# Two of a norm's modulation tiles multiplied on TensorE instead of VectorE, and small loads and position tables moved

## Chip, cores, metric

One NeuronCore of a Trainium2 chip. The metric is the device time of one execution in microseconds. Before the change: 3044.1 us, the median of 3 runs (3043.52 to 3049.18).

## What is computed

Two transformer blocks on 256 tokens of width 2048, in float32. The first block's modulation and first norm matter here:

```python
c_act = jax.nn.silu(c)
mod = (c_act @ ada_w[l] + ada_b[l]).reshape(B, N_MOD, D)[:, :, None, :]
shift_m, scale_m, gate_m, shift_f, scale_f, gate_f = [mod[:, i] for i in range(N_MOD)]
h = rmsnorm(x, norm_mix_g[l]) * (1.0 + scale_m) + shift_m
x = x + gate_m * token_mix(h, cos, sin, w_in[l], ...)
```

`c_act` is one vector of 2048; `ada_w` is 2048 by 12288. `shift_m` and `scale_m` are its first 4096 columns: eight tiles of 512. `cos` and `sin` come from `positions` and are used in the attention of `token_mix`. The second block attends to a memory `mem` of 256 rows, whose keys and values (`rmsnorm(mem) @ w_mem_kv`, one set for each of its two layers) the kernel computes first.

## The kernel before

The five engines run five programs that are written out by hand and wait for each other by semaphores. Activations lie with features on the partitions: `x`, `h_hi`, `h_lo` are [128, 16 chunks, 256 tokens].

**Weights.** All large weights pass in pieces of 1 MB (four chunks of 128 rows by 512 columns, or as much) through a ring of four slots, `w_raw`. SyncE issues the loads in the order of use; each waits (`free_slot`) until what lay in its slot has been consumed. The table `PRODUCTS` gives this order, and with it what each engine does: a product (`gla_q`, ...) is a matrix product of so many tiles of 512 columns, each of four pieces. A piece is cut in two by ScalarE (`w_hi`, a rounded copy, L1220, two halves of 1.05 us) and VectorE (`w_lo`, the rest, L1534), into two pairs of buffers; TensorE (all its matmuls pass through `mm`, L819) then makes three passes, hi by hi, lo by hi, hi by lo: 48 matmuls of 256 columns for a piece. A first cut can be put inside a norm that comes before it, by the table `CUT_IN_NORM` (norm, and chunk behind which piece e is cut).

**Modulation.** In mode "A" (`ada0`: three tiles, `ada1`: one) and as a rider between the pieces of other products, a piece of `ada_w` is multiplied by `c_act` on VectorE (`ada_piece`, L1584 and L1591, four operations of 128x512 for a piece, four pieces for a tile), into `probs_t`. `ada_total` on TensorE then sums it over the partitions by four matmuls of one column against ones, into PSUM `bank[3]`. `take_mod` (L1603) adds `ada_b`, `gain` (L1609) makes `gain_eff`. The first norm (called `mix`) needs the eight tiles 0 to 7: three of ada0, four riders on mem_k0, mem_v0, mem_k1, mem_v1, and ada1.

**The head, in order.** SyncE: `const` (L694), sixteen loads of small vectors into `vec_rows` (L705), `mem_rows`, `x_rows`, then the ring. POOL loads the positions. TensorE transposes `vec_rows` (L992), then `mem_rows` in four steps (`to_features`, L1003), sums the squares of the memory (norm mem0), transposes x in four steps, and goes to product mem_k0. ScalarE and VectorE copy the transposes out of PSUM. VectorE also makes the arguments of sine and cosine (`tables(0)`, L1782 to L1793; the sines are ScalarE's, L1362 and L1363) before its first copy. VectorE then multiplies four pieces of ada0, scales `mem_t` by the root (L1664), and in `apply("mem0")` writes `h_lo` two chunks at a time (L1668) with one of the other eight pieces of ada0 between them. Then follow the products mem_k0, mem_v0, (norm mem1) mem_k1, mem_v1 with a rider on each piece; behind them ada1, `take_mod(0, 8)`, `gain`, and `apply("mix")`, which writes h chunk by chunk (L1679, L1315 on ScalarE, L1687) with the first cuts of gla_q inside. Then gla_q, gla_gk (one piece), gla_k, and the rest of the two blocks.

Of the kernel before, what the change touches and what calls it, by code (L numbers as in the profile page):

```python
# [132 lines left out]
class Product:  # L133
# [18 lines left out]
    def ada_tiles(self, n):  # L152
# [36 lines left out]
CUT_IN_NORM = {"mem_k1": ("mem1", {0: -1, 1: -1, 2: 7, 3: 12}), "gla_q": ("mix", {0: 1, 1: 4, 2: 9, 3: 13}),  # L189
# [6 lines left out]
BEFORE = {"split": [0], "plain": [0], "ada": [0]}  # L196
_in_slot = [0] * 4
_p = _s = _t = _a = 0
for _i, _g in enumerate(PRODUCTS):

    _g.r0, _g.p0, _g.s0, _g.t0, _g.a0 = len(LANDED), _p, _s, _t, _a
    for _k in range(_g.tiles * _g.slots):
        _ada = _g.mode == "A" or (_g.rider > 0 and _k % (_g.rider + 1) == _g.rider)
        _in_slot[len(LANDED) % 4] += 16 * (1 if _ada else _g.dmas)
        LANDED.append(_in_slot[len(LANDED) % 4])
        KIND.append("ada" if _ada else "split" if _g.split else "plain")
        for _kind, _is in (("split", _g.split and not _ada), ("plain", not _ada), ("ada", _ada)):
            BEFORE[_kind].append(BEFORE[_kind][-1] + _is)
# [4 lines left out]
    _a += _g.ada_tiles(_g.tiles)  # L213
    _g.p1, _g.t1 = _p, _t
# [69 lines left out]
def program(nc, A, out):  # L284
    with ExitStack() as ctx:
# [124 lines left out]
        angles = at("angles", small[0] - 4 * KB, [P, 3, S])  # L410
# [61 lines left out]
        ada_done = sem("ada_done")  # L472
        ada_sum = sem("ada_sum")
# [137 lines left out]
        def ada_buffer(g, a):  # L611

            return a % 2 if g.rider == 1 else 0
# [78 lines left out]
        def _(sp):  # L692
            x_in, mem_in = A["x"][0], A["mem_2"][0]
            sp.dma_start(const[:], A["const"]).then_inc(ld_const, 16)  # L694
            n_vec = 0
            for name, (at0, w) in VECTORS.items():
                v = A[name]
                v = v.rearrange(" ".join(f"a{k}" for k in range(len(v.shape))) + " -> (" +
                                " ".join(f"a{k}" for k in range(len(v.shape))) + ")") if len(v.shape) > 1 else v
                v = v.rearrange("(r p) -> r p", p=P)  # L700
                done = 0
                while done < w:
                    r, t = (at0 + done) % P, (at0 + done) // P
                    n = min(P - r, w - done)
                    sp.dma_start(vec_rows[r:r + n, t, :], v[done:done + n]).then_inc(ld_vec, 16)  # L705
                    n_vec += 1
                    done += n
            assert n_vec == N_VEC_DMA
# [49 lines left out]
            for name in ("ada0", "mem_k0", "mem_v0", "mem_k1", "mem_v1", "ada1"):  # L758
# [32 lines left out]
        def _(pool):  # L791
# [21 lines left out]
            positions("positions_2")  # L813
# [3 lines left out]
        def _(pe):  # L817
# [61 lines left out]
            def ada_total(g, i, tb):  # L879

                a, n = g.a0 + tb // g.rider, g.ada_tiles(g.body)
                pe.wait_ge(ada_done, 4 * (a + 1) + per(i, 4 * n))
# [3 lines left out]
                last.then_inc(ada_sum, 1)  # L886

# [133 lines left out]
            product("mem_k0", *h, chunk_ready=as_normed("mem0"), between=[lambda: ada_total(G["ada0"], 0, 2)])  # L1021
# [1102 lines left out]
```

## Time and profile before

| | |
|---|---|
| time, median of 3 runs | 3044.1 us (3043.52 to 3049.18) |
| span of the profiled execution | 3058.3 us, 14.2 above that median; no other time of that execution is listed |
| TensorE busy, with matmuls | 2842.3 us, 93% |
| VectorE busy | 1830.9 us, 60% |
| ScalarE busy | 1196.0 us, 39% |
| mean granted TensorE clock | 0.961 of 2.4 GHz |
| modulation pieces on VectorE (L1591) | 360 operations, 270.2 us busy, 751 ns each |
| read from memory | 561.95 MB, 185 GB/s over the span |

The busy shares are means over the whole span; the first 7% of it, where the change lies, is different. PEld is TensorE's loading of weights, which overlaps its matmuls; an f32 matmul counts as two instructions in the profile. SPq is SyncE issuing a load. A PEclk of 0.50 is 1.2 GHz, 1.00 is 2.4 GHz.

### The profile page before, as it was taken

Reading aid. Unit: us, or ns where it says so; the run is one execution under the profiler, and the core shown is the slowest. Engines: PE = TensorE matmul, PEld = TensorE weight load, DVE = VectorE, ACT = ScalarE, POOL = GpSimd, SP = SyncE. Lnnn points to the kernel's source line nnn. Section 1 sums busy time; section 2 is a strip of 40 time slices with the busy share of each in tenths; the row PEclk is TensorE's granted clock in tenths of the full one; section 3 lists DMA queues with packets and bytes.
Section 4 is the critical chain, followed back from the end, with each engine's and each line's share of the span. In section 5 each row is a group of like instructions: output and inputs, shape, how many; then the busy total and the mean of one; then the engine's idle time right before and its main releaser. Section 6 shows DMA issues by size and latency. Waiting matters only on the chain.

```text
span 3058.3 us, 50651 instructions
## 1 busy us (share of the span) xinstructions
PE 2842.3 (93%) x21461; PEld 2720.1 (89%) x21461; DVE 1830.9 (60%) x2283; ACT 1196.0 (39%) x1508; POOL 5.7 (0%) x14
## 2 busy tenths in 40 slices
PE   3979988999999999989999999998997989899988
PEld 2879867999999779989999999997997989899888
DVE  6795665766765557764544444445556556646754
ACT  3435332343343433343333333333444344544533
POOL 0000000000000000000000000000000000000000
PEclk7989998999999979999999999998999999999988
DMA  7786822778767327745555555553553545654222
GB/s 266 280 305 232 289 91 70 260 250 284 253 235 210 90 101 257 260 162 196 176 182 183 184 183 178 178 180 110 180 186 127 174 142 189 197 179 152 83 84 95
DMA packets 319752, 568.32 MB, mean 186 GB/s; under 512 B 21961, under 2 KB 61217, under 8 KB 318962
## 3 DMA queue, kind: packets, MB, share of 16 engines
q1 hardware_dynamic: 318354, 561.73, 54.8%
q0 software_dynamic: 1248, 4.46, 0.4%
q8 instruction: 111, 1.82, 0.3%
q14 instruction: 39, 0.32, 0.0%
HBM read 561.95 MB, written 4.19 MB: 185 GB/s over the span
## 4 chain that ended last, share of the span: by engine, by line
PE 82%; DVE 13%; issue 3%; ACT 2%; DMA 1%; SPq 0%; DVEq 0%; ACTq 0%
PE tile_ps L819 74%; PE misc_ps L819 6%; DVE w_lo L1534 4%; DVE probs_t L1591 1%; ACT w_hi L1220 1%; DVE rstd L1641 0%; PE misc_ps L963 0%; DVE o_tmp L1978 0%; DVE stats L1753 0%; DVE x L1956 0%; DVE tile_ps L1874 0%; DVE gla_att L1877 0%; DVE o_lo L1738 0%; PE tile_ps L1003 0%; DMA w_raw<-in_w_mem_kv 0%
## 5 line engine op out<-in xcount | busy, mean ns | idle before, releaser
L1534 DVE TENSOR_TENSOR w_lo<-w_raw,w_hi 128x1024 fp32r<-128x1024 f32 x866 | 1021.4, 1221 | 890.1 <-ACT w_hi L1220 889.1
L1220 ACT ACTIVATE w_hi<-w_raw 128x1024 fp32r<-128x1024 f32 x866 | 867.7, 1050 | 1161.4 <-PE tile_ps L819 1120.2
L819 PE MATMUL tile_ps<-h_hi,w_hi 128*128 128x256 f32 x4208 | 695.9, 287 | 54.5 <-DVE w_lo L1534 33.5
L819 PE MATMUL tile_ps<-h_hi,w_lo 128*128 128x256 f32 x4208 | 687.3, 285 | 0.0
L819 PE MATMUL tile_ps<-h_lo,w_hi 128*128 128x256 f32 x4208 | 686.5, 284 | 0.0
L819 PEld LDWEIGHTS tile_ps<-h_hi,w_hi 128*128 128x128 f32 x4208 | 589.4, 193 | 64.5 <-issue 35.1
L819 PEld LDWEIGHTS tile_ps<-h_hi,w_lo 128*128 128x128 f32 x4208 | 587.7, 193 | 0.0
L819 PEld LDWEIGHTS tile_ps<-h_lo,w_hi 128*128 128x128 f32 x4208 | 587.6, 193 | 0.0
L1591 DVE SCALAR_TENSOR_TENSOR probs_t<-w_raw,c_act,probs_t 128x512 f32<-128x512 f32 x360 | 270.2, 751 | 10.9
L819 PE MATMUL tile_ps<-o_hi,w_hi 128*128 128x256 f32 x1024 | 168.5, 287 | 12.3 <-DVE w_lo L1534 7.5
L819 PE MATMUL tile_ps<-o_hi,w_lo 128*128 128x256 f32 x1024 | 166.2, 285 | 0.0
L819 PE MATMUL tile_ps<-o_lo,w_hi 128*128 128x256 f32 x1024 | 166.1, 285 | 0.0
L819 PEld LDWEIGHTS tile_ps<-o_hi,w_hi 128*128 128x128 f32 x1024 | 143.4, 195 | 14.9 <-DVE w_lo L1534 9.8
L819 PEld LDWEIGHTS tile_ps<-o_lo,w_hi 128*128 128x128 f32 x1024 | 142.9, 194 | 0.0
L819 PEld LDWEIGHTS tile_ps<-o_hi,w_lo 128*128 128x128 f32 x1024 | 142.9, 194 | 0.0
L819 PE MATMUL tile_ps<-sw_hi,w_hi 128*128 128x256 f32 x704 | 113.7, 284 | 1.7 <-DVE w_lo L1534 1.5
L819 PE MATMUL tile_ps<-sw_hi,w_lo 128*128 128x256 f32 x704 | 113.1, 283 | 0.0
L819 PE MATMUL tile_ps<-sw_lo,w_hi 128*128 128x256 f32 x704 | 113.1, 283 | 0.0
L819 PEld LDWEIGHTS tile_ps<-sw_hi,w_hi 128*128 128x128 f32 x704 | 97.1, 192 | 2.7 <-DVE w_lo L1534 2.7
L819 PEld LDWEIGHTS tile_ps<-sw_lo,w_hi 128*128 128x128 f32 x704 | 97.1, 192 | 0.0
L819 PEld LDWEIGHTS tile_ps<-sw_hi,w_lo 128*128 128x128 f32 x704 | 97.1, 192 | 0.0
L819 PE MATMUL tile_ps<-w_hi,h_hi 128*128 128x512 f32 x224 | 70.7, 397 | 0.0
(330 smaller groups left out, 2314.2 us busy)
## 6 DMA issues: line engine op xcount, KB each, us to landing
w_raw<-in_ada_w SPq DMA_DIRECT2D x96, 1024.0 KB, 5.2
w_raw<-in_w_in SPq DMA_DIRECT2D x89, 1024.0 KB, 5.1
w_raw<-in_ffn_w_in SPq DMA_DIRECT2D x88, 1024.0 KB, 5.0
w_raw<-in_w_out SPq DMA_DIRECT2D x48, 1024.0 KB, 5.1
w_raw<-in_ffn_w_down SPq DMA_DIRECT2D x44, 1024.0 KB, 5.1
w_raw<-in_b_w_in SPq DMA_DIRECT2D x33, 1024.0 KB, 5.2
w_raw<-in_a_w_in SPq DMA_DIRECT2D x32, 1024.0 KB, 5.5
w_raw<-in_w_kv SPq DMA_DIRECT2D x24, 1024.0 KB, 5.2
```

The costliest lines, as they stand in the source:

```text
L819: return nc.tensor.matmul(o, l, r, start=start, stop=stop, skip_group_check=True)
L1220: f(w_hi[s_ % 2][:, hf], w_raw[r % 4][:, hf], ACT.Copy).then_inc(cut_hi, 1)
L1534: ins = v.tensor_tensor(w_lo[s_ % 2][:, hf], w_raw[r % 4][:, hf], f32(w_hi[s_ % 2][:, hf]), ALU.subtract)
L1591: ins = v.scalar_tensor_tensor(acc, w[:, c, :], c_act[:, k:k + 1], acc, ALU.mult, ALU.add)
```

## The change

Two tiles, the first and the last of the eight, are multiplied on TensorE: `ada0` (one tile) at the start and `ada3` (one tile) behind mem_v1. A new function `ada_on_pe` uses the raw piece as weights and a column of `c_act` as the moving side, so that no sum over partitions is left: 16 matmuls of one column for a piece, accumulated in PSUM. A new semaphore `ada_by_pe` frees the ring's slots for them. The sixteen small loads move to ScalarE's queue, in front of all that ScalarE does. The first two pieces of mem_k0 are cut inside norm mem0, behind chunks 11 and 15. The tables move behind gla_q on VectorE and ScalarE, and `angles` gets a second place in memory. The modulation is taken in two steps, tiles 0 to 6 before the norm and tile 7 behind its chunk 11.

```diff
-PRODUCTS = [Product("ada0", 3, 4, split=False, mode="A", rider=1),
+PRODUCTS = [Product("ada0", 1, 4, split=False, mode="A", rider=1, on_pe=True),
+            Product("ada1", 1, 4, split=False, mode="A", rider=1),
             Product("mem_k0", 1, 4, rider=1), Product("mem_v0", 1, 4, mode="N", rider=1),
             Product("mem_k1", 1, 4, rider=1), Product("mem_v1", 1, 4, mode="N", rider=1),
-            Product("ada1", 1, 4, split=False, mode="A", rider=1),
+            Product("ada2", 1, 4, split=False, mode="A", rider=1),
+            Product("ada3", 1, 4, split=False, mode="A", rider=1, on_pe=True),
...
-CUT_IN_NORM = {"mem_k1": ("mem1", {0: -1, 1: -1, 2: 7, 3: 12}), "gla_q": ("mix", {0: 1, 1: 4, 2: 9, 3: 13}),
+CUT_IN_NORM = {"mem_k0": ("mem0", {0: 11, 1: 15}), "mem_k1": ("mem1", {0: -1, 1: -1, 2: 7, 3: 12}), "gla_q": ("mix", {0: 1, 1: 4, 2: 9, 3: 13}),
...
@@ the ring's free_slot, SyncE
-                                    ("plain", piece_done, g.body * g.kp), ("ada", ada_done, 4 * g.ada_tiles(g.body))):
+                                    ("plain", piece_done, g.body * g.kp), ("ada", ada_done, 4 * g.ada_tiles(g.body)), ("ada_pe", ada_by_pe, 0)):
...
@@ TensorE
+            def ada_on_pe(g, qs, dst):
+
+                for q in qs:
+                    r = ring(g, 0, q)
+                    pe.wait_ge(landed[r % 4], LANDED[r])
+                    w = w_raw[r % 4][:].rearrange("p (c n) -> p c n", c=4)
+                    for c in range(4):
+                        k = 4 * q + c
+                        for b in range(BLK):
+                            last = mm(dst[:, b:b + 1], w[:, c, b * P:(b + 1) * P],
+                                      c_act[:, k:k + 1], k == 0 and b == 0, k == DC - 1)
+                    last.then_inc(ada_by_pe, 1)
+                if q == 3:
+                    pe.wait_ge(ada_by_pe, BEFORE["ada_pe"][r + 1])
+                    pe.sem_inc(ada_sum, 1)
...
             for k in range(4):
                 to_features(k)
-            pe.wait_ge(vec_ready, 1)
+            pe.wait_ge(c_ready, 1)
+            ada_on_pe(G["ada0"], (0,), bank[3][:, 0:BLK])
             norm("mem0")
             for k in range(4, 8):
                 to_features(k)
+            ada_on_pe(G["ada0"], (1, 2, 3), bank[3][:, 0:BLK])
             for b in range(2):
                 pe.wait_ge(turn_out[b], 4)
-            ada_total(G["ada0"], 0, 0)
-            ada_total(G["ada0"], 0, 1)
...
             product("mem_v1", *h_mem)
-            for tb in range(G["ada1"].tiles):
-                ada_total(G["ada1"], 0, tb)
+            ada_total(G["ada2"], 0, 0)
+            ada_on_pe(G["ada3"], range(4), bank[2][:, 0:BLK])
             product("gla_q", *h, chunk_ready=as_normed("mix"))
...
@@ ScalarE: the loop over VECTORS, taken from SyncE, stands first in its program
+                    act.dma_start(vec_rows[r:r + n, t, :], v[done:done + n]).then_inc(ld_vec, 16)
...
             f(c_act[:], vec("c", 0, DC), ACT.Silu).then_inc(c_ready, 1)
-            tables(0)
             leave(0)
...
             product("gla_q", copy_to(pair(0), scale=GLA_DK ** -0.5))
+            tables(0)
             product("gla_gk", copy_to(lambda i, tb, g: gk_t[0:RANK, :], pre=[(gk_ones, 1)]))
...
@@ VectorE
-            early = [lambda tb=tb, q=q: ada_piece(G["ada0"], 0, tb, q) for tb in range(3) for q in range(4)]
-            for do in early[:4]:
-                do()
             sums("mem0")
-            apply("mem0", early[4:])
+            apply("mem0", [lambda q=q: ada_piece(G["ada1"], 0, 0, q) for q in range(4)])
...
-            take_mod(0, 2 * DC // BLK)
-            gain("norm_mix_g", 0, 1)
-            apply("mix")
+            take_mod(0, G["ada3"].a0)
+            gain("norm_mix_g", 0, 1, 0, 3 * BLK)
...
+            apply("mix", before={3 * BLK: last_scale})
```

On VectorE, between the scaling of `mem_t` and the first cut of mem_k0 (`w_lo`), the order before ends:

```order
L1668 SCALAR_TENSOR_TENSOR h_lo<-mem_t,cols,h_hi 128x256 [waits nm_hi] x2
L1591 SCALAR_TENSOR_TENSOR probs_t<-w_raw_51,c_act,probs_t 128x512 [waits ada_done,landed2]
L1591 SCALAR_TENSOR_TENSOR probs_t<-w_raw_51,c_act,probs_t 128x512 [waits ada_step] x3
L1668 SCALAR_TENSOR_TENSOR h_lo<-mem_t,cols,h_hi 128x256 [waits nm_hi] x2
L1591 SCALAR_TENSOR_TENSOR probs_t<-w_raw_52,c_act,probs_t 128x512 [waits ada_done,landed3]
L1591 SCALAR_TENSOR_TENSOR probs_t<-w_raw_52,c_act,probs_t 128x512 [waits ada_step] x3
L1534 TENSOR_TENSOR w_lo_55<-w_raw_49,w_hi_53 128x1024 [waits cut_hi] x2
```

and now:

```order
L1690 SCALAR_TENSOR_TENSOR h_lo<-mem_t,cols,h_hi 128x256 [waits nm_hi] x2
L1612 SCALAR_TENSOR_TENSOR probs_t<-w_raw_52,c_act,probs_t 128x512 [waits ada_done,landed3]
L1612 SCALAR_TENSOR_TENSOR probs_t<-w_raw_52,c_act,probs_t 128x512 [waits ada_step] x3
L1690 SCALAR_TENSOR_TENSOR h_lo<-mem_t,cols,h_hi 128x256 [waits nm_hi] x4
L1555 TENSOR_TENSOR w_lo_55<-w_raw_49,w_hi_53 128x1024 [waits cut_hi] x2
L1690 SCALAR_TENSOR_TENSOR h_lo<-mem_t,cols,h_hi 128x256 [waits nm_hi] x4
L1555 TENSOR_TENSOR w_lo_56<-w_raw_51,w_hi_54 128x1024 [waits cut_hi] x2
```

Ahead of the first cut stand eight pieces of modulation before and four now, and the cuts stand between the last chunks of the norm.

On TensorE, between the last matmuls of mem_v1 and the first of gla_q, before:

```order
L819 MATMUL tile_ps<-w_hi_54,mem_lo 128x512 x2
L819 MATMUL misc_ps<-const,probs_t 128x1 [waits ada_done]
L819 MATMUL misc_ps<-const,probs_t 128x1 x3
L819 MATMUL misc_ps<-const,probs_t 128x1 [waits ada_done]
L819 MATMUL misc_ps<-const,probs_t 128x1 x3
L819 MATMUL tile_ps<-h_hi,w_hi_53 128x256 [waits nm_lo,cut_lo,taken0]
```

and now:

```order
L810 MATMUL misc_ps<-const,probs_t 128x1 [waits ada_done]
L810 MATMUL misc_ps<-const,probs_t 128x1 x3
L810 MATMUL misc_ps<-c_act,w_raw_49 128x1 [waits landed0]
L810 MATMUL misc_ps<-c_act,w_raw_49 128x1 x15
L810 MATMUL misc_ps<-c_act,w_raw_50 128x1 [waits landed1]
L810 MATMUL misc_ps<-c_act,w_raw_50 128x1 x15
L810 MATMUL misc_ps<-c_act,w_raw_51 128x1 [waits landed2]
L810 MATMUL misc_ps<-c_act,w_raw_51 128x1 x15
L810 MATMUL misc_ps<-c_act,w_raw_52 128x1 [waits landed3]
L810 MATMUL misc_ps<-c_act,w_raw_52 128x1 x15
L810 MATMUL tile_ps<-h_hi,w_hi_53 128x256 [waits ada_by_pe,nm_lo,cut_lo,taken0]
```

Behind the sum of the last tile that VectorE multiplies stand 64 more matmuls of one column, and gla_q behind them.

## Rows read from the trace of the kernel before

**Rows 1.** Windows: PE, PEld, DVE, ACT, POOL busy, granted clock, DMA share, GB/s.
```profile
0.00:209.44 209.44, 133.19 (x772) 120.32 (x772) 162.21 (x223) 71.45 (x102) 2.99 (x9) 0.84 0.81 288
209.44:3058.30 2848.86, 2709.16 (x20690) 2599.74 (x20690) 1668.65 (x2061) 1124.53 (x1406) 2.72 (x5) 0.97 0.54 178
```

**Rows 2.** Chain that ended last: start us, us, what.
```profile
15.69 6.60 PE tile_ps L1003 x32
...
24.41 9.08 PE misc_ps L819 x32
...
36.61 1.95 ACT x L1369 x2
...
209.44 59.30 PE tile_ps L819 x480
```

**Rows 3.** Chain, timeline, and loads (KB each, us to landing), of the head.
```profile
1.21 0.42 SPq L705 DMA_DIRECT2D vec_rows<-in_norm_mix_g  x1
...
7.76 7.88 DMA mem_rows<-in_mem
...
const<-in_const SPq DMA_DIRECT2D x1, 447.0 KB, 3.2
...
9.27 0.81 PE L992 MATMUL misc_ps<-const,vec_rows 128*128 128x128 f32 x3 [9.27 <-DMA vec_rows<-in_cmp_pe]
...
w_raw<-in_w_in SPq DMA_DIRECT2D x89, 1024.0 KB, 5.1
```

**Rows 4.** Timeline, one-column sums: weight loads at the two clocks.
```profile
38.63 0.97 PEld L819 LDWEIGHTS misc_ps<-const,probs_t 128*128 128x128 f32 x8 [1.37 <-ACT x L1369]
...
202.24 1.78 PEld L819 LDWEIGHTS misc_ps<-const,probs_t 128*128 128x128 f32 x8 [7.46 <-DVE probs_t L1591]
```

**Rows 5.** Timeline, VectorE in norm mem0 and its first cut.
```profile
42.11 4.63 DVE L1664 TENSOR_TENSOR mem_t<-mem_t,rstd 128x1024 f32<-128x1024 f32 x4
...
50.20 0.88 DVE L1668 SCALAR_TENSOR_TENSOR h_lo<-mem_t,cols,h_hi 128x256 fp32r<-128x256 f32 x2
51.00 3.11 DVE L1591 SCALAR_TENSOR_TENSOR probs_t<-w_raw,c_act,probs_t 128x512 f32<-128x512 f32 x4
54.02 0.88 DVE L1668 SCALAR_TENSOR_TENSOR h_lo<-mem_t,cols,h_hi 128x256 fp32r<-128x256 f32 x2
...
76.65 2.35 DVE L1534 TENSOR_TENSOR w_lo<-w_raw,w_hi 128x1024 fp32r<-128x1024 f32 x2
```

**Rows 6.** Windows: clock after the transposes of x, transfers in mem_k0.
```profile
42.00:43.00 1.00, 0.00 (x0) 0.00 (x0) 0.97 (x2) 0.00 (x0) 0.00 (x0) 0.55 0.04 16
...
79.00:105.00 26.00, 25.94 (x203) 25.94 (x203) 22.87 (x29) 7.12 (x8) 0.00 (x0) 0.92 1.01 361
```

**Rows 7.** Timeline from the last modulation tile to gla_q.
```profile
204.14 0.19 DVE L1603 TENSOR_TENSOR mod<-misc_ps,cols 128x32 f32<-128x32 f32 x1 [1.96 <-PE misc_ps L819]
...
209.44 0.76 PE L819 MATMUL tile_ps<-h_hi,w_hi 128*128 128x256 f32 x2 [5.34 <-DVE w_lo L1534]
```

**Rows 8.** Windows: clock at the start of gla_q and in an attention.
```profile
209.00:212.00 3.00, 2.56 (x12) 2.59 (x13) 2.89 (x7) 1.82 (x3) 0.00 (x0) 0.50 1.04 358
212.00:215.00 3.00, 3.00 (x24) 3.00 (x24) 2.83 (x4) 1.52 (x4) 0.00 (x0) 0.87 1.04 398
...
1080.00:1104.00 24.00, 24.00 (x62) 14.17 (x62) 8.56 (x20) 5.84 (x23) 0.00 (x0) 0.50 0.00 0
```

**Rows 9.** Timeline, ScalarE: the sines, the cut of gla_k, a table load.
```profile
14.15 0.42 ACT L1362 ACTIVATE rope_sin<-angles 128x256 f32<-128x256 f32 x1 [3.20 <-DVE angles L1793]
14.47 0.49 ACT L1363 ACTIVATE rope_cos<-angles,stats 128x256 f32<-128x256 f32 x1
...
258.18 2.00 ACT L1220 ACTIVATE w_hi<-w_raw 128x1024 fp32r<-128x1024 f32 x2
263.02 0.37 ACT L1265 ACTIVATE gk_t<-tile_ps 16x256 f32<-16x256 f32 x1 [2.84 <-PE tile_ps L819]
...
271.34 1.28 ACT L1404 ACT_TABLE_LOAD   x1
```

More of the change, by code:

```diff
@@ L205 @@
         LANDED.append(_in_slot[len(LANDED) % 4])
-        KIND.append("ada" if _ada else "split" if _g.split else "plain")
-        for _kind, _is in (("split", _g.split and not _ada), ("plain", not _ada), ("ada", _ada)):
+        KIND.append(("ada_pe" if _g.on_pe else "ada") if _ada else "split" if _g.split else "plain")
+        for _kind, _is in (("split", _g.split and not _ada), ("plain", not _ada), ("ada", _ada and not _g.on_pe),
+                            ("ada_pe", _ada and _g.on_pe)):
             BEFORE[_kind].append(BEFORE[_kind][-1] + _is)
@@ L213 @@
     _a += _g.ada_tiles(_g.tiles)
+    _d += _g.ada_tiles(_g.tiles) * (not _g.on_pe)
     _g.p1, _g.t1 = _p, _t
@@ L611, in ada_buffer @@
         def ada_buffer(g, a):
-            return a % 2 if g.rider == 1 else 0
+            return (a - g.a0 + g.d0) % 2 if g.rider == 1 else 0
         def has_ada(g, q):
@@ L694, in _ @@
             sp.dma_start(const[:], A["const"]).then_inc(ld_const, 16)
[L695 to L708, printed above, removed]
             sp.dma_start(mem_rows[:], mem_in.rearrange("(t p) d -> p t d", p=P)).then_inc(ld_mem, 16)
@@ L756, in load @@
                                 load_ada(g, i, tb, q)
-            for name in ("ada0", "mem_k0", "mem_v0", "mem_k1", "mem_v1", "ada1"):
+            for name in ("ada0", "ada1", "mem_k0", "mem_v0", "mem_k1", "mem_v1", "ada2", "ada3"):
                 load(name)
@@ L1020, in _ @@
             as_normed = lambda n: (lambda k: [(nm_lo, N[n].c0 + k + 1)])
-            product("mem_k0", *h, chunk_ready=as_normed("mem0"), between=[lambda: ada_total(G["ada0"], 0, 2)])
+            product("mem_k0", *h, chunk_ready=as_normed("mem0"), between=[lambda: ada_total(G["ada1"], 0, 0)])
             product("mem_v0", *h, between=[lambda j=j: (sum_pair("mix", 2 * j), sum_pair("mix", 2 * j + 1)) for j in range(4)])
@@ L1209, in _ @@
             own = Steps(act, act_step)
+            n_vec = 0
+            for name, (at0, w) in VECTORS.items():
+                v = A[name]
+                v = v.rearrange(" ".join(f"a{k}" for k in range(len(v.shape))) + " -> (" +
+                                " ".join(f"a{k}" for k in range(len(v.shape))) + ")") if len(v.shape) > 1 else v
+                v = v.rearrange("(r p) -> r p", p=P)
+                done = 0
+                while done < w:
+                    r, t = (at0 + done) % P, (at0 + done) // P
+                    n = min(P - r, w - done)
+                    act.dma_start(vec_rows[r:r + n, t, :], v[done:done + n]).then_inc(ld_vec, 16)
+                    n_vec += 1
+                    done += n
+            assert n_vec == N_VEC_DMA
             f = nc.scalar.activation
@@ L1647, in sums, with apply @@
                     root_mean_square(n, rs, var[:], bank[0][:, 0:S])
-            def apply(name, between=()):
+            def apply(name, between=(), before={}):
                 n, between = N[name], iter(between)
@@ L1674, in apply @@
                 for c in range(n.n + 1):
+                    if c in before:
+                        before[c]()
                     if c < n.n:
@@ L1807, in _ @@
             dve.wait_ge(ld_const, 16)
-            tables(0)
             leave(1)
@@ L1825, in _, with last_scale @@
                     sums("mix")
-            for tb in range(G["ada1"].tiles):
-                for q in range(4):
-                    ada_piece(G["ada1"], 0, tb, q)
-            take_mod(0, 2 * DC // BLK)
-            gain("norm_mix_g", 0, 1)
-            apply("mix")
+            for q in range(4):
+                ada_piece(G["ada2"], 0, 0, q)
+            take_mod(0, G["ada3"].a0)
+            gain("norm_mix_g", 0, 1, 0, 3 * BLK)
+            def last_scale():
+                take_mod(G["ada3"].a0, 2 * DC // BLK, bank[2][:, 0:BLK])
+                gain("norm_mix_g", 0, 1, 3 * BLK, DC)
+            apply("mix", before={3 * BLK: last_scale})
             dve.wait_ge(nm_lo, N["mix"].c0 + DC)
@@ L1835, in _ @@
             product("gla_q")
+            tables(0)
             product("gla_gk")
@@ L1844, in _ @@
             product("gla_v")
-            take_mod(G["ada1"].a0 + 1, G["gla_g"].a0)
+            take_mod(2 * DC // BLK, G["gla_g"].a0)
             all_taken(dve, G["gla_v"])
```

50 lines of the change are left out of this document (26 added, 24 removed).

## Prediction

> **What bounds the kernel now.** I read the busy time of the engines in two stretches, then the chain that ended last, then the timelines around the places where it leaves TensorE. The stretches [rows 1] split the kernel at 209.44 us. Behind that point TensorE is busy 2709 of 2849 us; ahead of it only 133 of 209 us, VectorE 162. The chain [rows 2] says the same in order: a transfer, then short steps, then VectorE from 46.7 us on, then TensorE; from 209.44 us it runs through TensorE's matmuls without a gap. So the change, which touches little behind that point, is worth what it moves the start of product gla_q at 209.44 us. Two dates carry this: the start of product mem_k0 at 79.06 us, and the stretch from 202.24 us, when VectorE has ended the last modulation tile, to 209.44 us.
>
> The profiled execution has a span of 3058.3 us, 14.2 above the median of the runs, 3044.1; I sum against the span and carry the difference over to the median. About 0.2% (6.1 us) is what a measurement here tells from no change.
>
> **Change 1: the small loads leave SyncE's queue.** SyncE issues `const` and sixteen small loads before `mem_rows`, which is issued at 7.76 and lands 7.88 us later [rows 3]. Without the sixteen it is issued at 1.21, where the first of them stood. `const` (447 KB, landed 3.2 us after its issue as the first) is ahead of it, and 2 MB at the 400 GB/s or so of that stretch are 5.2 us, so it lands at about 9.3, 6.3 earlier. But TensorE first transposes the small vectors. ScalarE issues them at the same pace and so ends at 7.7 too; TensorE began them at 9.27 and needed 0.8 us [rows 3]. With `mem_rows` moving at the same time I allow 0.8 us more: the transposes of `mem_rows` begin at 10.9 instead of 15.69, 4.8 earlier. Bounds: 3 us (the small packets queue behind the large) and 6.3 us (nothing gets in their way).
>
> **Change 2: tile 0 on TensorE.** One tile is 64 matmuls of one column, and the trace shows four of them as eight weight loads: 0.97 us at the full clock, 1.78 us at 1.2 GHz [rows 4]. So 0.121 or 0.2225 us for each load and matmul, 128 of them for a tile: 15.5 or 28.5 us; a quarter of a tile 3.9 or 7.1. VectorE needs 3.11 us for a quarter [rows 5].
> - The first quarter stands between the transposes and the norm's sums. Its piece lands behind `x_rows`, at about 9.3 + 3 x 2.7 = 17.4 (1 MB at some 390 GB/s is 2.7 us; `x_rows` is two). Between 3.9 and 7.1 I take 5, since TensorE comes from the transposes without a pause: it ends at 22.5. The sums take 9.08 us and end at 31.6 instead of 33.5. Of the 4.8 us only 1.9 are left.
> - The other three quarters stand behind the transposes of x, which end at 35.6. In the trace the full clock lasted until 42.1, 4.6 us beyond their end at 37.5 [rows 6], so I take 3.9, 7.1 and 7.1: 39.5, 46.6, 53.7. Each frees a slot of `w_raw`, and the load into it lands 5.1 us later, the median of the ring's loads [rows 3]: 44.6, 51.7, 58.8.
> - VectorE no longer multiplies four quarters before the norm. They cost nothing now, since the norm's next step, the root at 38.6, waits for ScalarE's copies of x, which end at 36.61 + 1.95 [rows 2].
>
> **Change 3: half the quarters in the memory norm, and two cuts in it.** VectorE's scaling begins at 42.11 - 1.9 = 40.2 and ends at 44.8. Then it alternates two `h_lo` and one quarter every 3.82 us [rows 5]: eight quarters up to 76.6 before, four now. The quarters end at 48.7, 52.5 and 56.3; the fourth waits for its load (58.8) and ends at 61.9. Four more `h_lo` (1.6 us) end at 63.5. The first piece of mem_k0 is issued at 54 but moves behind the fourth ada1 piece, so it lands at 61.5; ScalarE's first half is done at 62.6, and VectorE's cut of 2.35 us runs 63.6 to 66.0. TensorE starts mem_k0 at 66.0 instead of 79.06: **13.1 us gained**. Bounds: 10 if all quarters on TensorE run at 1.2 GHz and the small loads come late, 16.4 if all run at full clock, when VectorE is never held and the cut ends at 62.6.
>
> The stretch from mem_k0 to the end of mem_v1 has the same instructions as before and its loads are released by the same events, so I move it as a whole. TensorE is the chain in mem_k0 and mem_v0; the two 1 MB loads that go with each piece (5.4 us) fit beside its 5.9 us of matmuls (48 of the 480 in 59.3 us [rows 2]), with little to spare.
>
> **Change 4: the last tile on TensorE.** Before, VectorE ends its last tile at 202.24, TensorE sums it, and `take_mod` starts at 204.14; gla_q starts at 209.44, 5.3 us later [rows 7]. That tile is still on VectorE (now called ada2), and only behind its sum does TensorE begin the 128 loads and matmuls of ada3. Nothing covers them: gla_q is behind them on the same engine, and VectorE must also wait, since the first cut of gla_q needs the slot that ada3's first quarter frees. TensorE has idled 7.5 us and is at 1.2 GHz: the eight at 202.24 took 1.78 us [rows 4]. Whether the clock rises is the question, and [rows 8] hold both answers: with the f32 matmuls of an attention back to back TensorE stayed at 1.2 GHz, fully busy, from 1080 to 1104 us; with the cut products of gla_q it went to 2.4 GHz 3.3 us after they began. The tile is f32, too, with a new weight load for each column, so it is nearer to the first, and I take 28.5 us. The other end is a rise after 3.2 us, as in gla_q: 14 of the 128 at 0.2225 and 114 at 0.121, 17.0 us. In both the norm's chunks are ready in time. Cost 28.5 - 5.3 = **23.2 us**.
>
> The Trainium skill says in TensorE: Matmul & The Clock Gate, section Why this matters for your kernels, that TensorE kept continuously busy leaves its slow clock. The attention of [rows 8] does not agree: busy without a pause, it stayed slow. By that rule the tile would take about 17 us and the sum would be that of rival A.
>
> **Change 5: the tables behind gla_q.** At the head VectorE's operations lay between TensorE's first transposes (10.1) and the first sine at 14.15 [rows 9], before `mem_rows` was there at 15.6: nothing is gained. Behind gla_q ScalarE gets, just before the cut for gla_k at 258.18, a table load (1.28) and two sines (0.42 and 0.49, overlapping to 0.8) [rows 9]. That cut must be finished by VectorE before TensorE ends gla_gk: 258.18 + 2.0 + 1.3 = 261.5 against 263.0, a slack of 1.5 us; 2.1 to 2.3 more leaves TensorE waiting about 0.7. Bounds: 0 and 2.3. VectorE's own 4 us at most fall into gla_q's last piece.
>
> **Sum.** -13.1 + 23.2 + 0.7 = +10.8: span 3069, time 3044.1 + 10.8 = **3054.9 us**, slower.
>
> **Rivals.**
> - **A, the clock rises in the one-column stream.** For it: the transposes of x were at full clock and the eight one-column matmuls behind them too. Against: the attention in [rows 8]. Then ada3 takes 17.0; cost 17.0 - 5.3 = 11.7, less 1.6 because gla_q no longer runs its first 3.3 us at half speed. The early quarters take 3.9 each: gain 16.4. With 0.7 for the tables and 0.4 for the fourth cut: -5.2, **3038.9**, faster than before; with the small loads unhindered 3037.4. It decides where the tile costs less than 16.4 + 5.3 - 0.7 = 21 us, or 164 ns for each load and matmul (17.7 us or 138 ns with the forecast's gain of 13.1). By the rule cited above from the Trainium skill it would come out this way.
> - **B, the head gives less.** The small loads wait behind `mem_rows` and all quarters are at 1.2 GHz: gain 10, +13.9, **3058.0**.
> - **C, the middle swallows a part.** The transfers are at their limit there (share 1.01, 361 GB/s in mem_k0 [rows 6]), so a start 13 us earlier finds its pieces late: with half the gain lost +17.3, **3061.4**. Against it: each load is released by the same engine steps as before.
> - **D, the change does not act**: 209.44 is set by something else, then 3044.1. The chain speaks against it.
>
> **How the numbers follow.** Forecast 0.62 (between 3051 and 3058), A 0.09, B 0.15, C 0.07, D 0.02, something between A and the forecast (the clock rises late in the tile) 0.05, around 3047. The range leaves out A, C and D, 0.18: 3046 to 3060. Slower by over 0.2%: the forecast almost whole, B, C: 0.80. Within 0.2%: half of A, D, the between case and a little of the forecast: 0.14. Faster: the rest of A, 0.06.
>
> **What would show it.** In the profile after: `mem_rows` landed near 9.3 and its transposes at 10 to 12; mem_k0 starting near 66; ada3's loads at 0.22 us each over 28 us with the granted clock at 0.5; gla_q starting near 219.7 instead of 209.44; one TensorE gap of under 1 us behind gla_gk. The prediction is wrong if the loads of ada3 fall to 0.12 us within some 5 us, or if mem_k0 starts outside 62 to 70.

## The result, and the profile after

The changed kernel takes **3065.9 us** (median of 4 runs, 3063.5 to 3069.2) beside 3046.6 for the kernel before, measured with it: 1.0060 times as long, interval 1.0048 to 1.0072. A second set of runs gave 3063.7 beside 3047.0, 1.0052 (1.0038 to 1.0066). So it is slower, by 16 to 19 us where I forecast 10.8, and above the upper end of my range, 3060.

The two stretches of [rows 1], split again at the start of gla_q (windows; us, then busy us of PE, PEld, DVE, ACT, POOL, then PEclk, DMA share, GB/s):

```profile
0.00:221.09 221.09, 174.57 (x1012) 162.49 (x1012) 145.38 (x199) 76.25 (x109) 2.98 (x9) 0.83 0.77 275
221.09:3061.50 2840.41, 2697.35 (x20690) 2591.16 (x20690) 1663.45 (x2054) 1121.50 (x1400) 2.71 (x5) 0.98 0.54 179
```

Ahead of gla_q VectorE lost 17 us of work, TensorE gained 41, and gla_q starts 11.7 us later (forecast 10.3). The chain of the changed kernel (start us, us, what), beside [rows 2]:

```profile
7.68 9.69 DMA vec_rows<-in_cmp_pe
...
23.83 12.42 PE misc_ps L810 x64
...
68.69 7.47 PE tile_ps L810 x48
...
191.61 29.19 PE misc_ps L810 x136
...
221.09 48.33 PE tile_ps L810 x384
...
276.15 5.99 PE tile_ps L810 x48
...
328.21 16.93 PE tile_ps L810 x74
```

It begins with a small load now. mem_k0 starts at 68.69 (before 79.06), the last VectorE tile ends at 191.61 (202.24), ada3 and the sum ahead of it take 29.19, gla_q starts at 221.09 (209.44), gla_v at 328.21 (314.80). The loads of the head (KB each, us from issue to landing) and TensorE's timeline, beside [rows 3]:

```profile
mem_rows<-in_mem SPq DMA_DIRECT2D x1, 2048.0 KB, 10.3
x_rows<-in_x SPq DMA_DIRECT2D x1, 2048.0 KB, 15.0
...
7.68 0.59 ACTq L1227 DMA_DIRECT2D vec_rows<-in_cmp_pe  x1
17.50 0.81 PE L999 MATMUL misc_ps<-const,vec_rows 128*128 128x128 f32 x3 [17.50 <-DMA vec_rows<-in_cmp_pe]
...
23.67 3.63 PE L810 MATMUL misc_ps<-c_act,w_raw 128*128 128x1 f32 x32
27.16 9.09 PE L810 MATMUL misc_ps<-nscratch_b,const 128*128 128x256 f32 x32
...
40.09 16.24 PE L810 MATMUL misc_ps<-c_act,w_raw 128*128 128x1 f32 x96
```

`mem_rows`, issued at 1.19, had landed at 11.5, but the last small load landed only at 17.4, 9.7 us after its issue, and TensorE wants it first. So the transposes of `mem_rows` began at 18.3, later than the 15.69 of before. The tile ada3 in TensorE's timeline, and two windows inside it, beside [rows 4, 8]:

```profile
193.34 27.45 PE L810 MATMUL misc_ps<-c_act,w_raw 128*128 128x1 f32 x128
...
196.00:200.00 4.00, 4.00 (x21) 4.00 (x20) 0.41 (x2) 0.00 (x0) 0.00 (x0) 0.50 1.05 402
...
212.00:216.00 4.00, 4.00 (x21) 4.00 (x20) 2.77 (x4) 2.40 (x3) 0.00 (x0) 0.50 0.18 33
```

Busy without a gap and at 1.2 GHz throughout: 27.45 us for the 128 loads and matmuls (64 matmuls of the program), 0.2145 us each where I had taken 0.2225. Last, the tables behind gla_q, beside [rows 9]:

```profile
270.48 1.28 ACT L1383 ACT_TABLE_LOAD   x1
271.77 0.42 ACT L1383 ACTIVATE rope_sin<-angles 128x256 f32<-128x256 f32 x1
272.10 0.49 ACT L1384 ACTIVATE rope_cos<-angles,stats 128x256 f32<-128x256 f32 x1
...
273.65 2.36 DVE L1555 TENSOR_TENSOR w_lo<-w_raw,w_hi 128x1024 fp32r<-128x1024 f32 x2 [3.04 <-ACT w_hi L1241]
...
276.15 0.71 PE L810 MATMUL tile_ps<-h_hi,w_hi 128*128 128x256 f32 x4 [1.00 <-DVE w_lo L1555]
```

The cut waits for ScalarE's table load and sines, and TensorE waits 1.0 us for the cut.

### The profile page after: what moved, and what is told of

Its sections match the earlier page's. It is cut to its first block, busy times and chain, and to the rows that moved or that the text cites. A ratio compares the mean times of both kernels' runs of the same rounds, so it can differ in the third digit from the quotient of the medians.

```text
span 3061.5 us, 51097 instructions
## 1 busy us (share of the span) xinstructions
PE 2871.9 (94%) x21701; PEld 2753.6 (90%) x21701; DVE 1808.8 (59%) x2253; ACT 1197.8 (39%) x1509; POOL 5.7 (0%) x14
## 4 chain that ended last, share of the span: by engine, by line
PE 82%; DVE 12%; issue 3%; ACT 2%; DMA 1%; ACTq 0%; DVEq 0%; SPq 0%
PE tile_ps L810 74%; PE misc_ps L810 7%; DVE w_lo L1555 4%; DVE probs_t L1612 1%; ACT w_hi L1241 1%; DVE rstd L1663 0%; DVE o_tmp L2003 0%; PE misc_ps L970 0%; DVE stats L1777 0%; DVE x L1981 0%; DVE tile_ps L1899 0%; DVE gla_att L1902 0%; DMA vec_rows<-in_cmp_pe 0%; DMA w_raw<-in_w_mem_kv 0%; DVE o_lo L1762 0%
## 5 line engine op out<-in xcount | busy, mean ns | idle before, releaser
L1612 DVE SCALAR_TENSOR_TENSOR probs_t<-w_raw,c_act,probs_t 128x512 f32<-128x512 f32 x330 | 247.8, 751 | 10.0
```

What stands on the lines that cost most here:

```text
L1612: ins = v.scalar_tensor_tensor(acc, w[:, c, :], c_act[:, k:k + 1], acc, ALU.mult, ALU.add)
```

## The experiments

All ratios are to the kernel before, run beside it on the same chip; before_again, loads_sp, ada3_dve and tables_head form one set, vec_after, warm, mixed and both_engines another, after_again, before_look and both_sp a third; changed and no_cuts have each their own. The starts are read from each chain.

| kernel | mem_k0 | gla_q | gla_v | rest | time (before) | ratio |
|---|---|---|---|---|---|---|
| before, shown first | 79.06 | 209.44 | 314.80 | 2743.5 | | |
| before_again | 76.70 | 206.62 | 311.88 | 2730.2 | 3048.8 (3049.8) | 1.0005 |
| before_look | 78.80 | 208.87 | 314.15 | 2728.9 | 3044.8, one run (3047.0) | |
| changed | 68.69 | 221.09 | 328.21 | 2733.3 | 3065.9 (3046.6) | 1.0060 |
| after_again | 71.06 | 223.15 | 330.28 | 2733.3 | 3063.7 (3047.0) | 1.0052 |
| loads_sp | 70.01 | 222.40 | 329.61 | 2733.3 | 3065.6 (3049.8) | 1.0056 |
| tables_head | 76.81 | 229.59 | 335.61 | 2737.8 | 3073.9 (3049.8) | 1.0078 |
| ada3_dve | 69.01 | 213.25 | 319.88 | 2736.0 | 3060.2 (3049.8) | 1.0036 |
| vec_after | 68.50 | 220.88 | 328.07 | 2733.3 | 3063.2 (3047.5) | 1.0047 |
| warm | 68.28 | 218.98 | 326.16 | 2733.3 | 3063.8 (3047.5) | 1.0053 |
| mixed | 68.33 | 224.26 | 330.68 | 2730.8 | 3067.0 (3047.5) | 1.0066 |
| both_engines | 67.82 | 199.45 | 306.07 | 2732.6 | 3043.0 (3047.5) | 0.9984 |
| both_sp | 69.91 | 199.91 | 305.20 | 2730.2 | 3038.6 (3047.0) | 0.9971 |
| no_cuts | 72.68 | 203.03 | 308.30 | 2730.2 | 3045.9 (3046.3) | 0.9996 |

"Rest" is the span less the start of gla_v. Intervals of the ratios reach 0.0009 to 0.0016 to either side, 0.0020 for warm and 0.0021 for mixed.

### The kernel before against itself

No edit.

> The kernel before, unchanged, measured against itself. It gives what two kernels of one program differ by, and a second profiled execution. Theory 1: the profiled execution that the sum was made against (span 3058.3 us) was an unlucky one; most executions have spans of 3040 to 3047 us, because TensorE's clock was low in fewer stretches, and the new profile shows where (attention of the MLA and of NSA). The start of gla_q stays at 209 to 210 us. Theory 2: runs of this program have the same stretches each time and the difference between span and time is what varies; then the new span is 3056 to 3060 again. Ratio 1.000 within 0.001.

> A third profile of the kernel before. What I want from it is how far the start of gla_q (209.4 and 206.6 us in the two so far) and the part behind gla_k (2743.5 and 2730.2 us) differ between executions of one program. If the first profile was the unlucky one: gla_q at 206 to 208; if both values are common, either.

The twelve runs lie between 3043.8 and 3059.8, and 17 of the same kernel beside them between 3041.4 and 3054.4, so theory 1 holds in its main point: the profile that I had summed against was of a long execution (span 3058.3; these two 3042.1 and 3043.0; the longest of the 29 is 3057.6). Two parts of it do not: 12 of the 29 spans, and not most, lie in 3040 to 3047, and gla_q started at 206.6, not at 209 to 210. The chain of before_again in the head and at gla_q:

```profile
23.62 7.52 PE misc_ps L819 x32
...
76.70 7.46 PE tile_ps L819 x48
...
206.62 59.19 PE tile_ps L819 x480
```

The norm's sums took 7.52 us where the first profile has 9.08 [rows 2] and the third 9.12. Further on the first profile lost most in an attention of the MLA. Its chain there, then that of before_again:

```profile
1096.83 5.16 PE misc_ps L819 x12
1101.98 0.62 PE misc_ps L963 x2
1102.60 4.30 PE misc_ps L819 x16
```

```profile
1089.05 3.46 PE misc_ps L819 x12
1092.51 0.37 PE misc_ps L963 x2
1092.89 2.36 PE misc_ps L819 x16
```

The same matmuls, for less of their time at the full clock in the one: the granted clock is 0.56 from 1092 to 1113 in the one, 0.80 from 1084 to 1100 in the other. Nothing else differs in the program.

### The changed kernel again

> The changed kernel again, for more executions beside the same executions of the kernel before, and a second profile. Theory 1 (the prediction missed because it was summed against one execution of the kernel before that was slow in its head and in its attentions): the difference to before is 15 to 18 us (ratio 1.005 to 1.006), gla_q starts at 219 to 222, the first 328 us are 13 to 16 us longer than before and the rest of the kernel takes the same 2730 to 2743 us. Theory 2 (the rest of the kernel is slower by the change, in the attentions or by the tables): the part behind 328 us is longer by 3 us or more than in the profiles of before.

Theory 1, with gla_q at 223.15 just outside its 219 to 222. Mean of the profiles: gla_v starts at 313.6 before, at 329.2 changed, **+15.6 us**. The spans of all runs average 3045.7 to 3048.1 before, by set, and 3060.8 and 3063.5 changed, some 16 more, so most of the difference arises ahead of gla_v. The rest of 2733.3 is 3 to 4 us above that of the two short profiles of before. It arises in the GLA (gated linear attention), where a step meets the low clock. The step 111.4 us behind the start of gla_v, in the changed kernel, in before_again, in both_engines and in both_sp:

```profile
439.62 4.50 PE tile_ps L810 x16
```

```profile
423.30 2.88 PE tile_ps L819 x16
```

```profile
417.49 4.55 PE tile_ps L816 x16
```

```profile
416.62 2.88 PE tile_ps L830 x16
```

Over the whole GLA the changed kernel lost 3.2 us to the low clock against before_again, and the first profile of before lost 4.2, at other steps. But this step does not go with the execution. It took 4.4 to 4.6 us in all eight profiles of kernels with the tables behind gla_q, and 2.88 in all six of kernels with the tables at the head. A later start is not the reason: in both_engines it begins at 417.5 and is slow, in before_again at 423.3 and is fast. The loads are not either: loads_sp has it slow with them on SyncE's queue. So of the change's parts it is the place of the tables that it goes with; how that acts on the clock some 170 us later is not shown.

### The small loads back on SyncE's queue

```diff
-                    act.dma_start(vec_rows[r:r + n, t, :], v[done:done + n]).then_inc(ld_vec, 16)
+                    sp.dma_start(vec_rows[r:r + n, t, :], v[done:done + n]).then_inc(ld_vec, 16)
```

> The changed kernel with its sixteen small loads back on SyncE's queue, ahead of mem_rows. Theory 1 (read from the profile after): on ScalarE's queue they gained nothing, since the last of them landed at 17.4 us behind the big transfers. Back on SyncE's queue the transposes of mem_rows begin at 15.7 instead of 18.1, but the first quarter of tile 0 waits for its piece, which lands behind x_rows at about 23 us; so mem_k0 starts at 68 to 69 and gla_q at 220 to 222, and the time is that of the changed kernel within 2 us. Theory 2 (the prediction's Change 1): the small loads on ScalarE's queue gain 1.9 us or more in the head; then gla_q starts at 223 or later here and the kernel is 2 us slower than the changed one.

Theory 1 in the time: 1.0056 against 1.0052 to 1.0060, no difference; mem_k0 (70.0) and gla_q (222.4) lie a little beyond its figures. Now the first quarter waits for its piece (chain):

```profile
8.84 14.32 DMA w_raw<-in_ada_w
23.29 14.30 PE misc_ps L824 x64
```

The quarter starts at 23.29 here and at 23.67 in the changed kernel, where its piece, issued at 2.17, was there at 19.5. The move of the loads traded one wait for another.

### The small transposes behind those of the memory

```diff
             for k in range(4):
                 to_features(k)
+            pe.wait_ge(ld_vec, 16 * N_VEC_DMA)
+            for t in range(3):
...
             pe.wait_ge(c_ready, 1)
             ada_on_pe(G["ada0"], (0,), bank[3][:, 0:BLK])
```

> The changed kernel with TensorE's three transposes of the small vectors (and their copy, and the silu of c) behind the four transpose steps of the memory instead of ahead of them. In the changed kernel mem_rows had landed at 11.5 us and waited for TensorE until 18.3, because the last small load landed at 17.4. Theory 1 (the head lost by order alone): the transposes of mem_rows begin at 11.6 and end at 18, the small ones follow, the first quarter of tile 0 begins at 19.5 to 20.5 instead of 23.7, and mem_k0 and gla_q start 3 to 4 us earlier (65 to 66, 217 to 218): 3 to 4 us faster than the changed kernel. Theory 2 (the transfers set the head, not the order): the first piece of w_raw or x_rows lands late enough, or the clock falls in the gap, that mem_k0 starts less than 1.5 us earlier.

Theory 2, and its reason is the clock. TensorE's timeline:

```profile
11.73 6.43 PE L1005 MATMUL tile_ps<-const,mem_rows 128*128 128x128 f32 x32 [11.73 <-DMA mem_rows<-in_mem]
...
20.15 6.44 PE L810 MATMUL misc_ps<-c_act,w_raw 128*128 128x1 f32 x32 [1.69 <-ACT c_act L1396]
26.45 9.65 PE L810 MATMUL misc_ps<-nscratch_b,const 128*128 128x256 f32 x32
```

The transposes begin 6.6 us earlier and the quarter 3.5, but it takes 6.44 us instead of 3.63 (0.20 us for each load and matmul, nearly the 0.2225 of 1.2 GHz), and the sums end at 36.1, where they end at 36.25 in the changed kernel. So with the wait for the small loads out of the way the head gained nothing in this profile; there is only the one.

### The tables back at the head

```diff
             f(c_act[:], vec("c", 0, DC), ACT.Silu).then_inc(c_ready, 1)
+            tables(0)
...
             product("gla_q", copy_to(pair(0), scale=GLA_DK ** -0.5))
-            tables(0)
```

> The changed kernel with the first position tables at the head again. Theory 1 (Change 5 of the prediction, mis-sized at 0.7): the tables behind gla_q cost 1.0 us of waiting before gla_k; without them that gap is gone and gla_k's first piece ends 1 us earlier after gla_q's start. In the head VectorE's 4 us of arguments stand between the copies of vec_rows and mem_rows and delay TensorE's third transpose step by 1.5 us, so gla_q starts 1 to 2 later and the time is unchanged within 1 us. Theory 2: the head hides them (VectorE idles 11 us before the root), then gla_q starts as in the changed kernel and the time is 1.0 to 1.8 us lower.

Worse than either theory: mem_k0 starts 5.8 to 8.1 us later, and the median is 8.3 us above that of loads_sp.

```profile
22.41 0.42 ACT L1383 ACTIVATE rope_sin<-angles 128x256 f32<-128x256 f32 x1 [3.19 <-DVE angles L1817]
...
24.19 3.67 PE L1010 MATMUL tile_ps<-const,mem_rows 128*128 128x128 f32 x16 [2.43 <-ACT mem_t L1390]
27.66 6.83 PE L810 MATMUL misc_ps<-c_act,w_raw 128*128 128x1 f32 x32
```

From gla_q to gla_v it takes 106.0 us instead of 107.1, so the gap of 1.0 is gone, as theory 1 had it; the head costs far more. With the small vectors there at 9.3 the sines end before `mem_rows` lands [rows 9]; with the vectors at 17.5 they stand in front of ScalarE's first copy. TensorE then idles 2.4 us, and the quarter behind it runs at half the pace. Moving the tables was the price of moving the loads.

### The last tile on VectorE

```diff
-            Product("ada3", 1, 4, split=False, mode="A", rider=1, on_pe=True),
+            Product("ada3", 1, 4, split=False, mode="A", rider=1),
...
-            ada_on_pe(G["ada3"], range(4), bank[2][:, 0:BLK])
+            ada_total(G["ada3"], 0, 0)
```

> The changed kernel with its last tile, ada3, on VectorE again. Theory 1: ada3 on TensorE costs 29.2 us of which VectorE's 12.7 us (4 quarters of 3.17) would remain, and 7.2 us from VectorE's end to gla_q: ada2 ends at 191.6 as now, ada3 at 204.3, gla_q starts at 211.5 instead of 221.1. The time falls by 9.6 us against the changed kernel, to about 3056, still 9 slower than before. Theory 2 (rival A, the clock would have risen if the stretch had been longer, or gla_q's loads and not TensorE set its start): gla_q starts less than 4 us earlier than in the changed kernel.

Theory 1, with 7.8 us instead of 9.6: VectorE's last quarters waited for their pieces and ended at 206.0 instead of 204.3. In time it is 5.4 us less than loads_sp, not 9.6. The kernel stays slower than before, so the engine is the smaller part of what the last tile costs. The larger part is its place: both_engines (below), with no second tile behind mem_v1 at all, starts gla_q at 199.45, 13.8 us ahead of this run, 1.2 of them from the head.

```profile
199.66 6.33 DVE L1612 SCALAR_TENSOR_TENSOR probs_t<-w_raw,c_act,probs_t 128x512 f32<-128x512 f32 x8 [1.07 <-DMA w_raw<-in_ada_w]
```

### Dense matmuls ahead of the last tile, and in it

warm, and mixed (inside `ada_on_pe`, for ada3 alone):

```diff
+            for j in range(64):
+                mm(bank[1][:, 0:S], mem_lo[:, j % 8, 0:P], mem_lo[:, j % 8, :], True, True)
             ada_total(G["ada2"], 0, 0)
```

```diff
                         for b in range(BLK):
                             last = mm(dst[:, b:b + 1], w[:, c, b * P:(b + 1) * P],
                                       c_act[:, k:k + 1], k == 0 and b == 0, k == DC - 1)
+                        if mix:
+                            mm(bank[1][:, 0:S], mem_lo[:, k % 8, 0:P], mem_lo[:, k % 8, :], True, True)
```

> The changed kernel with 64 dense matmuls (128 x 256, fp32r, on data that nobody needs, into a PSUM bank that nobody reads) in TensorE's queue between mem_v1 and the sum of ada2, so that TensorE comes into ada3 at 2.4 GHz. Output unchanged. Theory 1 (a one-column stream does not hold the clock, as after the transposes of x in the head, where 96 of these loads took 16.2 us and the clock fell about 5 us into them): the first 3 to 5 us of ada3 run at 0.11 us each, the rest at 0.22: ada3 takes 25 to 27 us instead of 28.5, gla_q starts 1.5 to 3.5 us earlier. Theory 2 (rival A with the right start: only the idle time ahead of ada3 kept the clock down): ada3 takes 15 us, gla_q starts 12 to 14 us earlier and the kernel is as fast as the one before or faster. Theory 3: the dense matmuls themselves end late and delay ada3 by more than they give.

> The changed kernel with one dense matmul (128 x 256, fp32r, into a PSUM bank that nobody reads) behind every four one-column matmuls of ada3, 32 in all. Output unchanged. If the clock stays at 1.2 GHz: 28.5 + 32 x 0.21 = 35 us, gla_q 6 to 7 us later than in the changed kernel. If the dense columns bring the clock up (theory: what lies in the stream decides, not how long it is): some 4 us at half speed, then 0.11 us each for 160 matmuls, about 20 us in all, gla_q 8 to 10 us earlier.

Timeline and windows of warm, then chain and a window of mixed:

```profile
185.12 7.91 PE L810 MATMUL misc_ps<-mem_lo 128*128 128x256 f32 x64
...
193.68 25.00 PE L810 MATMUL misc_ps<-c_act,w_raw 128*128 128x1 f32 x128
...
192.00:196.00 4.00, 4.00 (x38) 4.00 (x37) 2.43 (x7) 0.91 (x2) 0.00 (x0) 1.00 1.03 415
196.00:200.00 4.00, 4.00 (x23) 4.00 (x22) 0.74 (x2) 0.00 (x0) 0.00 (x0) 0.55 1.03 395
200.00:216.00 16.00, 16.00 (x77) 16.00 (x77) 8.44 (x13) 6.21 (x9) 0.00 (x0) 0.50 0.67 226
```

```profile
191.46 32.80 PE misc_ps L810 x152
...
208.00:216.00 8.00, 8.00 (x39) 8.00 (x39) 5.15 (x10) 3.65 (x6) 0.00 (x0) 0.50 0.40 133
```

The dense matmuls kept 2.4 GHz to the start of ada3, and the one-column stream lost it within 4 us of its start: 25.0 us for the tile instead of 27.45, theory 1. With one dense matmul in five the clock stayed at 0.50 to the end, and the tile with the sum ahead of it took 32.80 us, 3.6 more and not 6 to 7. The expectation had counted the dense ones double: a tile has 64 one-column matmuls, which the profile counts as 128, so there are 16 dense ones (152 = 8 + 128 + 16), and 16 x 0.21 is 3.4. Both speak against rival A: it is not the idle time before ada3 that keeps the clock down, it is the stream. The Trainium skill says in TensorE: Matmul & The Clock Gate, section Why this matters for your kernels, that continuous work brings the full clock; the 29.2 us of it in ada3 and its sum did not.

### The tiles divided anew

Tile 0 on TensorE, tile 1 on VectorE ahead of the root, tile 2 in the norm, one tile behind mem_v1:

```diff
-            Product("ada1", 1, 4, split=False, mode="A", rider=1),
+            Product("ada1", 2, 4, split=False, mode="A", rider=1),
...
-            Product("ada3", 1, 4, split=False, mode="A", rider=1, on_pe=True),
...
+HEAD = [("ada0", 0)] + [("ada1", q) for q in range(4)] + [("ada0", q) for q in (1, 2, 3)] + [("ada1", q) for q in range(4, 8)]
...
+            for q in range(4):
+                ada_piece(G["ada1"], 0, 0, q)
             sums("mem0")
-            apply("mem0", [lambda q=q: ada_piece(G["ada1"], 0, 0, q) for q in range(4)])
+            apply("mem0", [lambda q=q: ada_piece(G["ada1"], 0, 1, q) for q in range(4)])
```

> The tiles divided anew: tile 0 on TensorE as in the changed kernel, tile 1 on VectorE in the head ahead of the root (where VectorE idles from 25.1 to 36.4 us in the changed kernel), tile 2 on VectorE in the memory's norm, and only one tile behind mem_v1, on VectorE, as before; the ring's pieces in the order 0 | 1 1 1 1 | 0 0 0 | 2 2 2 2. Loads, cuts and tables as in the changed kernel. Theory 1 (the gain of the head is kept when no tile is pushed behind mem_v1): mem_k0 starts at 68 to 70 as in the changed kernel, the last VectorE tile ends at about 192, gla_q starts at 198.5 to 200 instead of 209.4, gla_k is 1.7 later by the tables: 8 to 9 us faster than before. Theory 2 (VectorE's idle time in the head is not free, since its pieces land late or the root is delayed): mem_k0 starts at 72 or later, and the gain is under 6 us.

> The tiles divided as in the run both_engines (tile 0 on TensorE, tile 1 on VectorE ahead of the root, tile 2 in the norm, one behind mem_v1), but the small loads on SyncE's queue and the tables at the head, both as before the change. If the loads and the tables of the change are worth nothing: transposes of mem_rows at 15.6, tile 0's first quarter at about 23.3 when its piece lands, mem_k0 at 67 to 70, gla_q at 199 to 202 and no gap behind gla_gk: the time of both_engines within 2 us, 4 to 7 us faster than before. If the loads on ScalarE's queue help with the tiles so divided, it is slower than both_engines by over 2 us.

Timeline of VectorE in both_engines, and the chains at gla_q, of both_engines and of both_sp:

```profile
25.84 11.98 DVE L1618 SCALAR_TENSOR_TENSOR probs_t<-w_raw,c_act,probs_t 128x512 f32<-128x512 f32 x15
37.73 0.42 DVE L1667 TENSOR_SCALAR var<-misc_ps 128x256 f32<-128x256 f32 x1
...
199.45 47.83 PE tile_ps L816 x384
```

```profile
199.91 59.23 PE tile_ps L830 x480
```

The four quarters ahead of the root fit into time in which VectorE idled, and gla_q starts 8.9 us ahead of the mean of before (208.3). both_engines is faster than before (0.9984, 0.9974 to 0.9994), by 4.5 us and not the 8 to 9 expected. So is both_sp, in which loads and tables stand where they stood: **0.9971 (0.9961 to 0.9982), 8.5 us less than before and 25 less than the changed kernel**. Between the two the medians differ by 4.4 us, more than the 2 expected, but they were timed on different chips and their intervals overlap, so which is faster is not settled. In the profiles both_sp is 0.9 us ahead at gla_v (the gap behind gla_gk less a later head) and 2.4 behind it, where the GLA step of 4.55 us in the one takes 2.88 in the other. Neither the moved loads nor the moved tables were needed for the gain.

### Without the cuts in the norm

```diff
-CUT_IN_NORM = {"mem_k0": ("mem0", {0: 11, 1: 15}), "mem_k1": ("mem1", {0: -1, 1: -1, 2: 7, 3: 12}), "gla_q": ("mix", {0: 1, 1: 4, 2: 9, 3: 13}),
+CUT_IN_NORM = {"mem_k1": ("mem1", {0: -1, 1: -1, 2: 7, 3: 12}), "gla_q": ("mix", {0: 1, 1: 4, 2: 9, 3: 13}),
```

> The kernel of the run both_sp without the two cuts of mem_k0 inside the memory's norm (the other part of Change 3). In both_sp VectorE cuts the first piece at 67.6, between the fourteenth and the last four h_lo, and mem_k0 starts at 69.9. Theory 1: without the cuts they follow the last h_lo: the four remaining h_lo (1.7 us) come first, mem_k0 starts 1.7 to 2.5 us later, at 71.6 to 72.4, and the kernel is 2 us slower than both_sp (some 6 to 7 us faster than before). Theory 2: what TensorE gains by starting early it spends waiting for the second piece, whose cut ScalarE and VectorE then do late; the times differ by under 1 us.

Theory 1, a little beyond its figures: the cut starts at 70.35 instead of 67.59, mem_k0 at 72.68, and gla_q 3.1 later. The ratio moved by 0.0025, about 7.5 us, of which the profiles (spans 3038.5 and 3035.4) show 3; the two were timed on different chips, and the excess stays open.

## Why the prediction was wrong

The direction and the largest term were right; the size was not. Two steps failed: Change 1, which priced the delay of the small vectors at 0.8 us where it was 8.2, and the base, one long execution taken for the kernel. Against its own profile the sum said +10.8 at gla_v and beyond, the trace has 328.21 - 314.80 = +13.4; the mean of the profiles +15.6.

- **Change 1 failed.** I had the transposes of `mem_rows` at 10.9, with bounds of 3 to 6.3 us of gain; they began at 18.3, a loss of 2.6. I said that TensorE takes the small vectors first, and allowed 0.8 us for their delay beside the big load. It was 8.2: TensorE began them at 17.50 instead of 9.27, since the last of them needed 9.7 us to land (17.4 less 7.7). The lower bound named this case, small packets behind large ones, and still called it a gain, although no row excluded a loss. Against before it costs little in the end, since with the loads on SyncE's queue the first quarter waits for its own piece until 23.3 (loads_sp); with them on ScalarE's that piece was there at 19.5.
- **Change 2.** The first quarter took 3.63 (forecast 5), the other three 16.24 (forecast 3.9 + 7.1 + 7.1 = 18.1). Right in kind, though its piece landed at 19.5 and not at 17.4. But the first quarter took 4.86 in the second profile of the same kernel, and 6.4 and 6.8 in vec_after and tables_head, behind pauses of TensorE of 1.7 and 2.4 us: it has no one price.
- **Change 3 was mis-sized by Change 1.** mem_k0 at 68.69 and 71.06 instead of 66.0, a gain of 10.4 against the first profile and 8.3 between the means (78.2 and 69.9), at and under my lower bound of 10. VectorE's scaling began at 44.86 instead of 40.2, and 2.0 of these 4.7 us came back, since its fourth quarter did not wait for a load as I had it; in the second profile it did wait. The cuts alone are worth about 2.8 of it (no_cuts). mem_k0 at 71.06 in the second profile is outside the 62 to 70 that I had named.
- **The middle as a whole: right.** From mem_k0 to the end of the last VectorE tile 122.9 us, before 123.2. Rival C is out.
- **Change 4: right.** From that end to gla_q 29.5 us instead of 7.2, a cost of 22.3 (forecast 23.2, with 28.5 for the tile that took 27.45), all 128 at 1.2 GHz. Rival A is out; neither a start at the full clock (warm) nor one dense matmul in five (mixed) brought it in.
- **Change 5 was too small.** From gla_q to gla_v 107.1 instead of 105.3: 1.8 us where I took 0.7, within the bounds. 1.0 is the gap; most of the other 0.8 is TensorE at 1.2 GHz for longer at the start of gla_q (granted clock 0.74 in its second 3 us, 0.94 before). Behind gla_v I put the tables at nothing; there one GLA step is 1.6 us longer in every profile with the tables behind gla_q, and the GLA as a whole 3.2 us longer than in four of the six without. "At the head nothing is gained" was right for before and wrong for the changed kernel, where gla_q starts 6 to 9 us later with the tables at the head (tables_head).
- **The base.** I summed against one execution with a span of 3058.3 and carried the sum to a median of three runs, 3044.1. The five sets of its runs had medians of 3046.3 to 3049.8. So of the miss of 11.0 us 2.5 are that base (3046.6 less 3044.1), 2.6 the terms (13.4 less 10.8), 2.2 that the first profile of before was slow in its head and that of the changed kernel quick (15.6 less 13.4), and the last 3.7 belong to no step for certain. The GLA's 3 us are of that size, but before loses as much to the low clock in some of its executions, and the second set put the median of the changed kernel 2 lower. Of the rivals B was nearest: a head that gives less, at 3058.0. Of its two conditions the small loads did come late, but the quarters did not all run at 1.2 GHz.

The change fails for a plain reason that both_sp shows. It took a tile from VectorE ahead of the norm, where VectorE had idle time that hid it, and gave a tile to TensorE behind mem_v1, where nothing hides it.

## What to carry to other kernels

Ask of each piece of work that moves to another engine whether it was hidden where it stood: four quarters on VectorE in the head cost nothing, and 64 one-column matmuls ahead of the next product cost all their 27.5 us. Bound a load by the last thing that its consumer waits for, not by the largest, and let the bound reach below zero where no row forbids it. And where run times of one program lie 10 us apart, take the base from several executions before adding terms of a few us to it. When a difference behind the change looks like chance, compare all profiles: the slow GLA step stood in all eight with the tables moved and in none of the six without.

## What the runs showed of the hardware that I had not expected

- Small loads issued on a second queue by 8.3 us landed behind the large ones: 32 KB took 9.7 us while 2 MB issued at 1.19 needed 10.3. The Trainium skill says in Trainium Kernel Development and Optimization, section Key Constraints, that the queues share the same 16 DMA engines and interleave, and that issuing from several engines saves only issue time. These runs agree in that the second queue gained nothing: 1.0056 with them on SyncE's queue, 1.0052 and 1.0060 without.
- A stream of one-column f32 matmuls, each with its own weight load, does not keep the clock: at 1.00 when it started, 0.55 in the window from 2.3 to 6.3 us behind its start, 0.50 from there (warm), and with 16 dense matmuls among the 64 it never rose (mixed).
- Executions of one program differ by where they meet the low clock: 34.8 us for the attention at 1078 in one, 28.6 at 1071 in the other, and spans from 3041.8 to 3057.6 in twelve runs. Not all of it is chance: one step of the GLA is slow in every profile with the position tables behind gla_q, 4.4 to 4.6 us instead of 2.88.
